# Queries and Fourier inputs in pairs by seven products, values of the latent groups between the first parts of scores, and one modulation tile later

## The chip, the cores and the metric

The kernel runs on one core of one Trainium2 chip, in float32 throughout. The metric is the device time in microseconds of one execution; the time before is the median of three runs.

## The reference

Two models of two layers each run one after the other on 256 tokens of width 1024. The first ("a") has attention, an mLSTM, cross attention and gated FFNs with a short convolution. The change touches almost only the second ("b"), and of it the projections and the attention. In layer 0 of b the latent tokens (256) and the context tokens (256) both go through it, so that its matmuls have 512 columns; in layer 1 only the latent ones ask for queries.

```python
h = modulate(x, lp["g_norm1"], sh1, sc1)
hc = modulate(xc, lp["g_norm1"], modc[..., :d], modc[..., d:2 * d])
proj = h @ lp["w_in"]
projc = hc @ lp["w_in"][:, :n_in_c]
...
c_q, q_g = jnp.split(qc, [MLA_Q_RANK], axis=-1)
q_mla = (rms_norm_2(c_q, lp["g_cq"]) @ lp["w_uq"]).reshape(b, l, MLA_HEADS, MLA_QK)
q_gqa = rms_norm_2(q_g.reshape(b, l, GQA_HEADS, GQA_DIM), lp["g_qn_gqa"])
...
o_mla = blocked_attend(q_mla, jnp.concatenate([k_mla_c, k_mla_l], axis=1),
                       jnp.concatenate([v_mla_c, v_mla_l], axis=1), MLA_QK ** -0.5)
o_gqa = blocked_attend(q_gqa, jnp.concatenate([k_gqa_c, k_gqa_l], axis=1),
                       jnp.concatenate([v_gqa_c, v_gqa_l], axis=1), GQA_DIM ** -0.5)
o_four = fourier_mix(proj[..., FOUR_START:GATE_START])
```

`mod = silu_c @ w_mod + b_mod` gives the shifts, scales and gates of a layer. Its weights are independent of everything in model a.

## The kernel before

The program is one long list of parts, written out by hand; each part names what TensorE, ScalarE, VectorE and GpSimd do in it, and an engine does its pieces in the order of the list. An engine's wait therefore holds up everything behind it on that engine. Results hand over by counters: `tick` raises an engine's counter when an instruction ends, `of` gives the value that a reader waits for.

PSUM has eight banks of 512 float32 columns. Whoever fills a bank again calls `claim(pe, bank)` first, which waits for the labels that the last user left by `lend(bank, ...)`, that is, for its readers.

Weights stream in slabs of up to 32 tiles (128x128) through two slots in turn. SyncE asks for slab g when slab g-2 has been used. `next_tiles` hands the tiles out, and the matmul that ends a slab ticks it.

A linear job (`tensor_linear`, L569) makes 128 output features of 512 columns: eight matmuls, one for each 128 of the 1024 inputs. In the trace each matmul of the program has two records. The first b layer's queries are the jobs 0 to 10 of `q0`: 0 to 2 make the low-rank query (`CQ`), 3 to 6 the grouped queries, of which ScalarE makes the squares (L1561) and VectorE the copy with its gain (`query_reads`, L2343); 7 to 10 are the Fourier inputs, which ScalarE copies half of and VectorE folds (`fold_reads`, L2352 and L2354). The jobs go round the banks 0 to 3. After job 3 the norm of `CQ` (`qnorm0`, L518 to L508) stands on VectorE. Behind `q0` comes `tensor_low` (L2448), which claims banks 0 to 3 in turn.

The merge of this layer, and the FFNs, already multiply a 2x2 block of weights with a 2x2 block of tokens by seven products in place of eight, with sums of weights (GpSimd, L2944; VectorE, L2921 and L2923) and sums of tokens (L2884 and on). A merge unit is one pair of output features (L2799).

The attention of b (`tensor_pairs`, `scalar_pairs`, `vector_pairs`, with the stage names `batt0` and `batt1`) works in units of a pair of heads by 128 queries. Units from `plain` on are the latent ones with rope and go in groups of four score parts (`scores_of_four`, L1356 and L1359), two units u and u+1 at a time. The chain of a unit is: scores on TensorE (banks 2*(u%2) and the next), minima on VectorE, `exps` on ScalarE (L1430), reciprocal and product on VectorE, `turn` on TensorE (L1372, banks 4 and 5), `copy_t` on ScalarE and VectorE (L1448), `values` on TensorE (L1384), and `output` on ScalarE (L1440). The values of a unit go to bank 6 or 7 by the parity of its output number `out`; two units share an output in some families (`out_first`, `out_last`). The first of an output claims the bank, which is lent by the copy of the output two before it. Behind the groups comes a `late` part, the late gate's matmuls (L2784), on TensorE, then the last turns and values.

At the start, `vector_mod_tiles` makes the products for the modulation (L612, two for each tile) between other work of VectorE; each waits for its weights (two transfers of 512 KB) to land in one of three buffers. L1935 (VectorE) and L1947 (TensorE) make the lambda of model a's attention. The tiles 7 and on stand in the jobs of `foxin`, the projection of the first a layer.

## Time and profile before

| | |
|---|---|
| Median of 3 runs | 2502.84 us (2501.11 to 2503.05) |
| The profiled execution | 2505.26 us, span 2503.5 us |
| TensorE busy | 2453.6 us, 98% of the span |
| VectorE, ScalarE, GpSimd busy | 1335.4, 548.7 and 621.4 us |
| Granted TensorE clock, mean | 0.998 |

The span is from the first to the last instruction of the profiled execution; the device time of that execution is 1.8 us longer, and it was 2.4 us slower than the median of the others. TensorE is the engine that the others serve, so a wait on it is time, while waits elsewhere are not.

### The profile page before, as it was taken

To read this page: it belongs to the slowest core of one execution; us is meant where nothing else is said; L and a number is where in the kernel's file an instruction comes from. 1 tells how busy PE (TensorE), PEld (TensorE's weight loads), DVE (VectorE), ACT (ScalarE), POOL (GpSimd) and SP (SyncE) were. 2 spreads that over 40 slices of the span, in tenths; PEclk is the share of its full clock that TensorE was granted. 3 is DMA by queue.
4 is the path that set the end of the run, shared out by engine and by line. 5 is a ranking of instruction groups with operands and counts; after the bars stand their busy time and mean duration, and the time that the engine had idled before them with its cause. 6 is when DMAs were issued, how large, how long until landed. Compare 5 with 4: busy or idle time off the path is not lost.

```text
span 2503.5 us, 37953 instructions
## 1 busy us (share of the span) xinstructions
PE 2453.6 (98%) x14528; PEld 2024.2 (81%) x14528; DVE 1335.4 (53%) x2707; ACT 548.7 (22%) x1199; POOL 621.4 (25%) x536
## 2 busy tenths in 40 slices
PE   9999999999999999999999999999999999999999
PEld 6757889996799999645567767888888875899999
DVE  6676467741325776324836763545542247435775
ACT  2132122111212221214620002222200215212220
POOL 1101135420212544001012221333241010232543
PEclk9999999999999999999999999999999999999999
DMA  8745344433333453120024662121222120243453
GB/s 313 284 186 201 127 162 153 193 131 135 117 135 119 168 193 135 66 87 26 2 84 156 218 260 88 68 101 71 110 93 80 68 95 26 104 166 153 168 193 110
DMA packets 39128, 334.67 MB, mean 134 GB/s; under 512 B 3920, under 2 KB 9168, under 8 KB 21712
## 3 DMA queue, kind: packets, MB, share of 16 engines
q1 hardware_dynamic: 32080, 307.61, 33.0%
q0 software_dynamic: 6912, 25.17, 2.7%
q8 instruction: 95, 1.56, 0.2%
q14 instruction: 41, 0.34, 0.0%
HBM read 331.72 MB, written 1.05 MB: 133 GB/s over the span
## 4 chain that ended last, share of the span: by engine, by line
PE 89%; DVE 5%; DMA 3%; issue 2%; ACT 1%; POOL 1%; SPq 0%; DVEq 0%; POOLq 0%; ACTq 0%
PE PS L767 25%; PE PS L569 15%; PE PS L1016 11%; PE PS L2799 6%; PE PS L1583 4%; PE PS L1743 4%; PE PS L2840 4%; PE PS L1728 3%; PE PS L2318 2%; PE PS L1384 2%; PE PS L1372 1%; DMA arena<-in_mod 1%; PE PS L436 1%; DMA slot<-in_weights 1%; PE PS L748 1%
## 5 line engine op out<-in xcount | busy, mean ns | idle before, releaser
L569 PE MATMUL PS<-XN,slot 128*128 128x256 f32 (+1 forms) x1184 | 296.8, 411 | 0.8 <-DVE XN L508 0.8
L767 PE MATMUL PS<-SQ,slot 128*128 128x128 f32 (+1 forms) x1984 | 294.4, 301 | 1.8 <-DVE slot L859 1.8
L569 PEld LDWEIGHTS PS<-XN,slot 128*128 128x128 f32 x1184 | 224.4, 190 | 69.8 <-issue 42.5
L767 PEld LDWEIGHTS PS<-SQ,slot 128*128 128x128 f32 x1984 | 268.1, 191 | 14.9 <-DVE slot L859 2.0
L1016 PE MATMUL PS<-arena,slot 128*128 128x128 f32 (+1 forms) x1902 | 251.5, 293 | 3.7 <-DVE arena L1094 2.2
L767 PE MATMUL PS<-XN,slot 128*128 128x128 f32 (+1 forms) x1664 | 250.0, 301 | 0.0
L1016 PEld LDWEIGHTS PS<-arena,slot 128*128 128x128 f32 x1902 | 239.1, 192 | 13.5 <-DVE arena L1094 2.8
L767 PEld LDWEIGHTS PS<-XN,slot 128*128 128x128 f32 x1664 | 226.1, 192 | 10.7
L886 DVE SCALAR_TENSOR_TENSOR arena<-PS,small,arena 128x255 f32<-128x255 f32 (+2 forms) x352 | 174.8, 544 | 44.7 <-ACT arena L830 44.1
L830 ACT ACTIVATE arena<-PS,small 128x256 f32<-128x256 f32 (+1 forms) x176 | 105.3, 617 | 399.3 <-DVE PS L919 238.9
L612 DVE CUSTOM_DVE_ANT_0 arena<-arena 128x1024 f32<-128x1024 f32 x80 | 107.3, 1382 | 30.2 <-DMA arena<-in_mod 30.2
L2799 PE MATMUL PS<-arena,slot 128*128 128x256 f32 (+1 forms) x704 | 119.7, 328 | 1.7 <-DVE slot L2923 1.7
L2799 PEld LDWEIGHTS PS<-arena,slot 128*128 128x128 f32 x704 | 107.0, 191 | 11.8 <-DVE slot L2923 2.4
L446 ACT ACTIVATE SQ<-X 128x512 f32<-128x512 f32 (+1 forms) x68 | 36.1, 552 | 364.1 <-DVE X L1058 93.1
L767 PE MATMUL PS<-SQ,probs 128*128 128x128 f32 (+1 forms) x704 | 111.4, 301 | 1.3 <-DVE SQ L871 1.3
L2944 POOL TENSOR_TENSOR slot<-slot 128x512 f32<-128x512 f32 x22 | 30.0, 1364 | 328.9 <-DMA slot<-in_weights 328.9
L612 DVE CUSTOM_DVE_ANT_1 arena<-arena,X 128x1024 f32<-128x1024 f32 x80 | 92.9, 1219 | 33.7 <-DMA arena<-in_mod 33.7
L1743 PE MATMUL PS<-arena,slot 128*128 128x128 f32 (+1 forms) x688 | 110.1, 321 | 0.0
L937 POOL TENSOR_TENSOR slot<-slot 128x512 f32<-128x512 f32 x84 | 108.4, 1291 | 0.0
L1743 PEld LDWEIGHTS PS<-arena,slot 128*128 128x128 f32 x688 | 101.4, 191 | 8.4 <-issue 0.5
L949 POOL TENSOR_TENSOR arena<-arena 128x256 f32 (+3 forms) x88 | 80.6, 916 | 102.6 <-ACT arena L839 102.6
L767 PEld LDWEIGHTS PS<-SQ,probs 128*128 128x128 f32 x704 | 97.7, 191 | 6.0 <-DVE SQ L871 1.5
(302 smaller groups left out, 3828.2 us busy)
## 6 DMA issues: line engine op xcount, KB each, us to landing
slot<-in_weights SPq DMA_DIRECT2D x85, 2048.0 KB, 7.8
slot<-in_weights SPq DMA_DIRECT2D x16, 2816.0 KB, 9.7
slot<-in_weights SPq DMA_DIRECT2D x24, 1536.0 KB, 6.8
arena<-in_mod POOLq DMA_DIRECT2D x48, 512.0 KB, 6.5
arena<-in_mod SPq DMA_DIRECT2D x48, 512.0 KB, 3.3
slot<-in_weights SPq DMA_DIRECT2D x5, 1024.0 KB, 5.5
slot<-in_weights SPq DMA_DIRECT2D x2, 2176.0 KB, 8.4
arena<-in_c SPq DMA_DIRECT2D x2, 1024.0 KB, 12.0
```

The costliest lines, as they stand in the source:

```text
L569: mm = pe.matmul(o, l, r, start=k == 0, stop=k == len(terms) - 1, skip_group_check=True)
L612: return dve.tensor_tensor_reduce(scratch, w, c, 1.0, 0.0, ALU.mult, ALU.add, total)
L767: mm = pe.matmul(PS[:, bank, 0:h], lhs[:, k * P:(k + 1) * P], rhs(k), start=first and k == 0, stop=last and k == 3, skip_group_check=True)
L830: act.activation(hb[:, half, :], src[half], ACT.Identity, bias=conv_col(s, m - 1, half, 3), scale=conv_col(s, m - 1, half, centre))\
L886: op = dve.scalar_tensor_tensor(out=o[:, :, lo:hi], in0=x[:, :, lo + d:hi + d], scalar=conv_col(s, m - 1, half, c), in1=o[:, :, lo:hi], op ...
L937: pool.tensor_tensor(a21, a11, a21, ALU.subtract).then_inc(*w_tick(s, GD, "s3", i, turn))
L949: pool.tensor_tensor(dst, hb[:, 0, :], hb[:, 1, :], ALU.mult).then_inc(*w_tick(s, GD, "h", i, turn))
L1016: mm = pe.matmul(d_psum(p, what, h), lhs[:, k * P:(k + 1) * P], rhs(k), start=k == 0, stop=k == KH - 1, skip_group_check=True)
L1583: mm = pe.matmul(PS[:, bank, 0:cols_n], lhs(k, t), r, start=k == 0, stop=k == k_tiles - 1)
L1743: mm = pe.matmul(PS[:, bank_of(m), part[g]], w[:, a:a + P], rhs(k, part[g]), start=k == 0, stop=k == k_tiles - 1, skip_group_check=True)
L2799: mm = pe.matmul(PS[:, bank, 0:hq], lhs[:, k * P:(k + 1) * P], rhs[:, k, 0:hq], start=first and k == 0, stop=last and k == 3, skip_group_c ...
L2840: mm = pe.matmul(PS[:, BBR + i, 0:nq], slot[:, a:a + P], BR[b][:, k, 0:nq], start=k == 0, stop=k == 3, skip_group_check=True)
```

## The change

There are four edits in one.

1. The modulation tile 7 leaves the start and goes into the `foxin` jobs: `range(0, 7)` there, `range(7, 16)` here.
2. The jobs 5 to 10 of `q0` become three pairs of two output features of 512 columns each, by seven products of four matmuls with 256 columns. GpSimd adds s1 and s3 of each pair's weights in the slab, VectorE s2 and s4; the token sums t1 to t4 are made once by VectorE, ahead of the reads of the first job. Bank 0 or 1 (`ba`) and 2 or 3 (`bd`) hold the products that end in PSUM, 4, 5 and 7 the others. `c12` is made in PSUM, and the reads of the upper job come from bank `ba`, those of the lower one from SBUF. The slab of `q0`'s first jobs is cut short and each pair has a slab of 16 tiles.
3. On TensorE, in both b attentions: the values of u-4 stand between the first score part of u and that of u+1 in each latent group; before, the values of u-2 stood behind the turn of u-1.
4. On ScalarE the output copies follow: those of u-4 and u-3 stand at the end of a group, where those of u-3 and u-2 stood.

```diff
             def scores_of_four(u):
                 for p, rope in enumerate(zip(units[u]["rope"], units[u + 1]["rope"])):
                     for v in (u, u + 1):
+                        if p == 0 and v > u:
+                            values(u - 4)
                         for i in range(2):
                             if p == 0:
                                 claim(pe, 2 * (v % 2) + i)
...
                 turn(u - 2)
-                if u == plain:
-                    values(u - 4)
                 values(u - 3)
                 turn(u - 1)
-                values(u - 2)
-            if plain == n:
-                values(n - 4)
-            else:
+            values(n - 4)
+            if plain < n:
                 late(pe)
...
                 copy_t(u - 1)
-                if u == plain:
-                    output(u - 4)
+                output(u - 4)
                 output(u - 3)
-                output(u - 2)
             copy_t(n - 2)
-            if plain == n:
-                output(n - 4)
+            output(n - 4)
...
-                add(scalar=lambda a: scalar_silu_c(a, 0), vector=lambda d: vector_mod_tiles(d, *range(0, 8)),
+                add(scalar=lambda a: scalar_silu_c(a, 0), vector=lambda d: vector_mod_tiles(d, *range(0, 7)),
...
-                        vector_mod_tiles(dve, *{2: range(8, 16), 6: range(16, 23)}.get(j, ()))
+                        vector_mod_tiles(dve, *{2: range(7, 16), 6: range(16, 23)}.get(j, ()))
...
-                jobs = feature_jobs(xq, lambda k: None, 11, q_reads, segs=qseg)
+                jobs = feature_jobs(xq, lambda k: None, 5, q_reads, segs=qseg)
+                Q_PAIRS = 3
...
+                def tensor_query_pairs(pe, s=s):
...
+                        ba, bd = i % 2, 2 + i % 2
+                        pe.wait_ge(sem, landed)
+                        claim(pe, ba)
+                        product(a11, XQ[:, :, 0, 0:T], ba, last=False).then_inc(*tick(TD, s, "p1", i))
+                        pe.wait_ge(*of(s, "sums", i))
...
+                        claim(pe, 4)
+                        product(s2, TQ[:, 1], 4).then_inc(*tick(TD, s, "p6", i))
+                        claim(pe, 5)
+                        product(s3, TQ[:, 2], 5).then_inc(*tick(TD, s, "p7", i))
+                        claim(pe, bd)
+                        product(s1, TQ[:, 0], bd, last=False).then_inc(*tick(TD, s, "p5", i))
+                        claim(pe, 7)
+                        product(a22, TQ[:, 3], 7).then_inc(*tick(TD, s, "p4", i))
+                        pe.wait_ge(*of(s, "p1_copied", i))
+                        product(a12, XQ[:, :, 1, 0:T], ba, first=False)
+                        pe.wait_ge(*of(s, "c22", i))
+                        product(s4, XQ[:, :, 1, T:2 * T], bd, first=False)\
+                            .then_inc(*tick(TD, "slab", first_slab["pairs0"] + i))
...
+                        lend(ba, (s, "c12", i), *[(s, "read", 5 + 2 * i, r) for r in range(len(upper))])
+                        lend(bd, (s, "c12", i))
...
+                def vector_query_pair(dve, i, s=s):
...
+                    dve.wait_ge(*of(s, "p3", i))
+                    dve.tensor_tensor(PS[:, i % 2, T:2 * T], PS[:, bd, 0:T], Q_U2, ALU.add).then_inc(*tick(VD, s, "c12", i))
+                    for part, made in zip((1, 0), ("c21", "c12")):
+                        dve.wait_ge(*of(s, made, i))
+                        for r, (_, op) in list(enumerate(pair_reads(i)[part]))[1:]:
+                            op(dve).then_inc(*tick(VD, s, "read", 5 + 2 * i + part, r))
```

TensorE at the end of the first jobs of `q0`, before: job 4 (its first row waits for VectorE) and behind it the jobs 5 and 6 in other banks.

```order
L569 MATMUL PS<-XN,slot 128x512 [waits vector_done]
L569 MATMUL PS<-XN,slot 128x512 x7
L569 MATMUL PS<-XN,slot 128x512 [waits scalar_done]
L569 MATMUL PS<-XN,slot 128x512 x7
L569 MATMUL PS<-XN,slot 128x512 [waits vector_done]
L569 MATMUL PS<-XN,slot 128x512 x7
```

The same place after, with lines moved by 6: job 4, then the first products of pair 0 (L2423 is the matmul of `product`).

```order
L575 MATMUL PS<-XN,slot 128x512 [waits vector_done]
L575 MATMUL PS<-XN,slot 128x512 x7
L2423 MATMUL PS<-XN,slot 128x256 [waits vector_done,scalar_done,landed1]
L2423 MATMUL PS<-XN,slot 128x256 x3
L2423 MATMUL PS<-arena,slot 128x256 [waits vector_done]
L2423 MATMUL PS<-arena,slot 128x256 x3
L2423 MATMUL PS<-arena,slot 128x256 [waits vector_done]
L2423 MATMUL PS<-arena,slot 128x256 x3
```

Job 5 waited for ScalarE alone there; the first product of pair 0 waits for VectorE, ScalarE and the landing of its own slab. The last product of pair 2, and the first matmuls of `tensor_low` (now L2581) behind it:

```order
L2423 MATMUL PS<-XN,slot 128x256 [waits vector_done]
L2423 MATMUL PS<-XN,slot 128x256 x3
L2581 MATMUL PS<-arena,slot 128x512 [waits vector_done,scalar_done,landed0]
L2581 MATMUL PS<-arena,slot 128x512
L2581 MATMUL PS<-arena,slot 128x512 [waits vector_done,scalar_done]
```

TensorE in the group of units 16 and 17 of `batt0`, before: the turn of unit 13, the values of unit 12 (L1384 from `probs_t`), then the first score parts of 16 and of 17 (L1356).

```order
L1372 MATMUL PS<-small,probs 128x128 [waits vector_done,scalar_done]
L1372 MATMUL PS<-small,probs 128x128 x3
L1372 MATMUL PS<-small,probs 128x128 [waits vector_done]
L1372 MATMUL PS<-small,probs 128x128 x3
L1384 MATMUL PS<-probs_t,arena 64x128 [waits scalar_done,vector_done]
L1384 MATMUL PS<-probs_t,arena 64x128 x7
L1356 MATMUL PS<-arena 128x256 [waits scalar_done]
L1356 MATMUL PS<-arena 128x256
L1356 MATMUL PS<-arena 128x256 [waits scalar_done]
L1356 MATMUL PS<-arena 128x256
L1359 MATMUL PS<-arena 128x256 x4
```

The same place after (L1380, L1392 and L1364 are the former L1372, L1384 and L1356): the turn, the first part of 16, the values of 12, the first part of 17.

```order
L1380 MATMUL PS<-small,probs 128x128 [waits vector_done,scalar_done]
L1380 MATMUL PS<-small,probs 128x128 x3
L1380 MATMUL PS<-small,probs 128x128 [waits vector_done]
L1380 MATMUL PS<-small,probs 128x128 x3
L1364 MATMUL PS<-arena 128x256 [waits scalar_done]
L1364 MATMUL PS<-arena 128x256
L1392 MATMUL PS<-probs_t,arena 64x128 [waits scalar_done,vector_done]
L1392 MATMUL PS<-probs_t,arena 64x128 x7
L1364 MATMUL PS<-arena 128x256 [waits scalar_done]
L1364 MATMUL PS<-arena 128x256
L1367 MATMUL PS<-arena 128x256 x4
```

The values of unit 12 have gone from in front of the scores of 16 to in front of those of 17. ScalarE in the group of units 14 and 15, before: copy of the turned unit 12, exponentials of 14 and of 15, turned copy of 13, output copy.

```order
L1448 ACTIVATE probs_t<-PS 128x512 [waits tensor_done]
L1430 ACTIVATE probs,pair_sum<-PS,pair_min,query_rstd 128x512 [waits vector_done,tensor_done]
L1430 ACTIVATE probs,pair_sum<-PS,pair_min,query_rstd 128x512
L1430 ACTIVATE probs,pair_sum<-PS,pair_min,query_rstd 128x512 [waits vector_done,tensor_done]
L1430 ACTIVATE probs,pair_sum<-PS,pair_min,query_rstd 128x512
L1448 ACTIVATE rms<-PS 128x512 [waits tensor_done]
L1440 ACTIVATE arena<-PS 128x256 [waits tensor_done]
```

The same place after (L1452, L1434 and L1444 are the former L1448, L1430 and L1440); this output copy is now the one of unit 10, which the values of unit 12 claim their bank from. Before, it was done a group earlier.

```order
L1452 ACTIVATE probs_t<-PS 128x512 [waits tensor_done]
L1434 ACTIVATE probs,pair_sum<-PS,pair_min,query_rstd 128x512 [waits vector_done,tensor_done]
L1434 ACTIVATE probs,pair_sum<-PS,pair_min,query_rstd 128x512
L1434 ACTIVATE probs,pair_sum<-PS,pair_min,query_rstd 128x512 [waits vector_done,tensor_done]
L1434 ACTIVATE probs,pair_sum<-PS,pair_min,query_rstd 128x512
L1452 ACTIVATE rms<-PS 128x512 [waits tensor_done]
L1444 ACTIVATE arena<-PS 128x256 [waits tensor_done]
```

## Rows read from the trace of the kernel before

**Rows 1.** The page: busy time by engine, and the chain that ended last
```profile
PE 2453.6 (98%) x14528; PEld 2024.2 (81%) x14528; DVE 1335.4 (53%) x2707; ACT 548.7 (22%) x1199; POOL 621.4 (25%) x536
...
PE 89%; DVE 5%; DMA 3%; issue 2%; ACT 1%; POOL 1%; SPq 0%; DVEq 0%; POOLq 0%; ACTq 0%
```

**Rows 2.** Timeline of PE, the start (start, length, engine, line, [wait before <-releaser])
```profile
1.46 5.37 PE L2988 MATMUL PS<-rms 128*128 128x512 f32 x6 [1.46 <-DVE rms L3001]
...
68.67 0.35 PE L1947 MATMUL PS<-tiny,small 128*128 128x2 f32 x2 [1.81 <-DVE tiny L1935]
...
158.18 1.13 PE L1344 MATMUL PS<-arena,small 128*128 128x256 f32 x4
```

**Rows 3.** Timeline of DVE (VectorE), the start up to the first attention
```profile
68.36 0.16 DVE L1935 TENSOR_TENSOR tiny<-small 128x2 f32<-128x2 f32 x1
...
153.08 1.23 DVE L612 CUSTOM_DVE_ANT_1 arena<-arena,X 128x1024 f32<-128x1024 f32 x1 [5.98 <-DMA arena<-in_mod]
...
154.24 1.22 DVE L612 CUSTOM_DVE_ANT_1 arena<-arena,X 128x1024 f32<-128x1024 f32 x1
...
159.96 0.29 DVE L1486 CUSTOM_DVE_ANT_0 probs<-PS,small 128x128 f32<-128x128 f32 x1
```

**Rows 4.** Timeline of PE, queries and Fourier inputs, first b layer
```profile
1070.55 48.23 PE L569 MATMUL PS<-XN,slot 128*128 128x512 f32 x112
1118.62 7.03 PE L2448 MATMUL PS<-arena,slot 128*128 128x512 f32 x16
```

**Rows 5.** Timeline of PE, one merge unit and the gate behind it
```profile
1416.91 1.89 PE L2799 MATMUL PS<-XN,slot 128*128 128x256 f32 x8
...
1428.99 7.03 PE L2840 MATMUL PS<-SQ,slot 128*128 128x512 f32 x16
```

**Rows 6.** Timeline of DVE, queries and Fourier inputs
```profile
1071.48 3.35 DVE L521 RECIPROCAL probs_t<-SQ 128x512 f32<-128x512 f32 x1
...
1079.04 1.40 DVE L2343 TENSOR_SCALAR arena<-PS,small 128x512 f32<-128x512 f32 x2
...
1098.70 0.42 DVE L2352 TENSOR_TENSOR arena<-PS,arena 128x256 f32<-128x256 f32 x1 [5.90 <-ACT arena L1561]
```

**Rows 7.** The page: POOL's (GpSimd's) sums, and a weight slab's issue to landing
```profile
L2944 POOL TENSOR_TENSOR slot<-slot 128x512 f32<-128x512 f32 x22 | 30.0, 1364 | 328.9 <-DMA slot<-in_weights 328.9
...
slot<-in_weights SPq DMA_DIRECT2D x5, 1024.0 KB, 5.5
```

**Rows 8.** Timeline of DVE, the first merge unit
```profile
1273.86 0.68 DVE L2921 TENSOR_TENSOR slot<-slot 128x512 f32<-128x512 f32 x1
...
1296.52 0.43 DVE L2915 TENSOR_TENSOR PS<-PS,arena 128x256 f32<-128x256 f32 x1 [3.03 <-PE PS L2799]
```

**Rows 9.** Timeline of PE, groups of four, first b layer's attention
```profile
1211.73 1.13 PE L1356 MATMUL PS<-arena 64*128 64x512 f32 x4 [1.47 <-ACT probs L1430]
...
1227.34 0.70 PE L1356 MATMUL PS<-arena 64*128 64x256 f32 x4 [0.51 <-ACT probs L1430]
...
1242.77 2.34 PE L1356 MATMUL PS<-arena 64*128 64x512 f32 x8
...
1251.41 0.70 PE L1356 MATMUL PS<-arena 64*128 64x256 f32 x4 [0.51 <-ACT probs L1430]
```

**Rows 10.** Timeline of ACT (ScalarE), output copies, first b layer's attention
```profile
1227.57 0.39 ACT L1440 ACTIVATE arena<-PS 128x256 f32<-128x256 f32 x1
...
1244.21 0.66 ACT L1440 ACTIVATE arena<-PS 128x256 f32<-128x256 f32 x2
```

**Rows 11.** Timeline of PE, groups of four, second b layer's attention
```profile
2103.86 1.13 PE L1356 MATMUL PS<-arena 64*128 64x512 f32 x4 [0.80 <-ACT probs L1430]
...
2132.13 1.09 PE L1384 MATMUL PS<-probs_t,arena 128*64 128x128 f32 x16
2133.15 3.72 PE L2784 MATMUL PS<-XN,slot 128*128 128x256 f32 x16
```

**Rows 12.** Timeline of ACT, the output copy before the late gate's end
```profile
2134.58 0.39 ACT L1440 ACTIVATE arena<-PS 128x256 f32<-128x256 f32 x1
```

109 lines of the change are left out of this document (104 added, 5 removed).

## Prediction

> **What bounds the kernel now.** I read the page first. TensorE is busy for 98% of the span and carries 89% of the chain that ended last [rows 1]: time is saved only by taking matmuls away from TensorE or by shortening one of its few waits, and every new wait on it is paid in full, unless it eats one that stood behind it. Then I read TensorE's timeline at the four places that the change touches, then VectorE's and ScalarE's rows at the same places, because each wait there ends with a semaphore of one of those two, and last the order of instructions, to see behind what the released instruction now stands.
>
> **Part A, the moved modulation tile.** At 68.67 TensorE waited 1.81 us for the small product at L1935 on VectorE [rows 2], which started at 68.36, directly behind the last modulation tile [rows 3]. A tile is two instructions of the kind at 153.08 and 154.24, which start 1.16 apart, so 2.3 us [rows 3]. With tile 7 gone from there the product comes 2.3 us sooner and the wait of 1.81 goes whole: at most -1.8. But VectorE is then one tile behind until it catches up. Up to the first attention it does not: the tiles are bound by their landings, and the last group (tiles 30 to 32) starts when it has waited 5.98 us for a landing, at 153.08, and ends as the first minimum of the attention starts, at 159.96 [rows 3]. The scores that this minimum reads ended at about 159.3 (158.18 + 1.13) [rows 2]. Now the group is four tiles if the landings don't come sooner: the minimum would be at about 162.2, +2.3; if they come sooner (their buffers and the queue follow TensorE's slabs, which are 1.8 earlier), it is at about 158.3 and all is kept. Both ends: -1.8 and +0.3 (a part of the lag is absorbed, as attention's first exponentials hold two units of scores in reserve). I take **-1.0**, past the middle towards the gain, since nothing shows the landings to be late by themselves.
>
> **Part B, three pairs by seven products.** Before, seven jobs took 48.07 us, from 1070.55 to 1118.62 [rows 4], 6.87 each, so the six that are replaced took 41.2. A pair does 7 products x 4 matmuls with 256 columns each, exactly what a merge unit does between its start at 1416.91 and its next other work at 1428.99 [rows 5]: 12.08 us, three times 36.24. Gain of matmul time: **-4.96**.
>
> What is given back at the seams. *Entry:* the first product of pair 0 claims bank 0, which job 4, the matmuls just before it, filled. Bank 0 is free when VectorE has read it, and that read (the second of the two at 1079.04, ending 1080.44) stands behind the norm of the queries: the reciprocal of 3.35 us from 1071.48 and what follows it [rows 6]. Job 4's matmuls end 6.87 after 1070.55, at 1077.42. So TensorE stands 3.0 us and some semaphore time: **+3.1**. Before, job 5 went to another bank and nobody noticed. *Exit:* the low-rank stage at L2448 started without a wait [rows 4], because the last job was in bank 2; its first matmul wants bank 0, which pair 2 (banks 0 and 2) lends when its last sum c12 is made in PSUM (0.43, as at 1296.52 [rows 8]) and when VectorE, behind the two folds of the lower job, has done the two of the upper (folds of 0.42, as at 1098.70, starting 0.35 apart [rows 6]): 0.2 to notice + 4 x 0.35 + 0.42 = **+2.05**. *Inside the pairs* nothing waits: GpSimd's two sums are 1.36 us each [rows 7] and VectorE's two 0.69 each [rows 8], under 5 us in all against 12.08 of matmuls, and the slab of 16 tiles (1024 KB, 5.5 us to landing [rows 7]) is asked for when the slab two before is done, 12 us or more ahead. If that cover were gone, a pair would pay up to the 5.5. For pair 0 the two sums stand behind the same reads, and are ready at 1080.44 + 1.4 = 1081.9, while the first product runs until 1080.5 + 1.7 = 1082.2: just hidden, by 0.3. The four token sums (four of the 128x1024 kind, 1.2 us each by the tile rows [rows 3]) go to VectorE between 1055 and 1061, where it had nothing to do before the first query read. Part B: -4.96 + 3.1 + 2.05 = **+0.2**. So what seven products save is paid at the two seams.
>
> **Part C, values of the latent groups, first attention.** The values of unit u-4 now stand between the first part of the scores of u and that of u+1. The second part waits for the exponentials of u-1, since they free its banks: 1.47 at 1211.73 and 0.51 at 1227.34 and 1251.41 [rows 9]. In the first group of four this fills a wait: values of 1.02 in place of standing, but ScalarE then becomes the next bound, so I take **-0.65** of the 1.47 (0 and -1.0 as ends). In the later groups the same work only changes its side of the wait, so nothing is gained. And the output copies on ScalarE have moved too: the copy of unit u-4 now stands behind both exponentials and the turned copy of its group. Three of the moved values (units 12, 16, 18) are the first of their output bank and claim it: they wait for the copy of units 10, 14 and 16. In the program the claim asks for a later ScalarE count than the second part of the scores does. Where was that copy in time? In the trace of before the copy that stands in the same place, behind exponentials and turned copy, ended at 1227.57 + 0.39 = 1227.96; at the second place there are two in one row at 1244.21, of which the first, the one that is waited for, ends after the same 0.39, at 1244.60 [rows 10]. Then the values need 1.02 (from 2132.13 to 2133.15 [rows 11]), with 0.07 of semaphore, and the scores behind them start at 1229.06, against 1227.34; at the second place at 1245.7, against 1243.95, where the second half of the row at 1242.77 began (2.34 long, 0.12 of it wait) [rows 9]; the third, at 1251.41, repeats the first. **+1.7 three times, +5.2.** The price is that of a matmul group behind a claim on the engine's one queue: the scores, the ropes and both turns of the group are queued behind it, and ScalarE's next exponentials wait for them, so nothing gives it back. Part C: **+4.6** (ends -0.65 and +5.2).
>
> The Trainium skill ("Perfetto Trace Analysis", the section on a TensorE instruction's phases) says that TensorE's queue can pull weight loads ahead of matmuls in flight and reorders nothing else; by it the scores can't pass the values that wait. If they could, the term of 5.2 would be nothing and the sum 1.2. The trace agrees as far as it can: the matmul row at 1211.73 stands 1.47 with all that is behind it.
>
> **Part D, the second attention.** The first group gains out of the wait of 0.80 at 2103.86 [rows 11]: -0.55, and two small waits of 0.12 are filled, or not: I give +0.24 for them on account of the output copies. Its values of unit 12 stood in front of the late gate's matmuls at 2133.15 [rows 11] and now stand behind a claim that is released by the copy at 2134.58 + 0.39 = 2134.97 [rows 12]: + 1.02 + 0.07 = 2136.07 against 2133.15, **+2.9**. The late gate follows it and waits too. Part D: **+2.6** (ends -0.35 and +2.9).
>
> **The sum.** -1.0 + 0.2 + 4.6 + 2.6 = +6.4. It is made in the profiled execution, 2505.26 us, which is 2.4 above the median of the runs (2502.84); put on the median it gives **2509.2** (0.26% slower). Its own range is 2506.5 to 2511.5: A between -1.8 and +0.3, C and D together within 1.5. I call 0.2% (5.0 us) what a measurement of this kernel can tell.
>
> **The rivals.** *No late outputs:* if the copies don't hold the values up (ScalarE reaches them sooner, because its exponentials start sooner once the first part of the scores is no longer behind values), C and D are -0.65 and -0.35: -1.0 + 0.2 - 1.0 = -1.8, 2501.0. For it: the first part of the scores does start 1.02 sooner. Against: the exponentials of u-1, which are what ends last, hang on the group before and not on it. *Half of it:* the copies cost in the first attention alone or with half the price: -1.8 + 2.9 to -1.8 + 5.2, 2504 to 2506.5. *Hand-over free, faster:* a single mechanism, banks given back before they are asked for, at the seams of the pairs as well as for the outputs: -1.0 - 4.96 - 1.0 = -7.0, 2495.9. It decides from the point at which VectorE's read of job 4 ends before 1077.4; it ended at 1080.44, and for that the norm of the queries would have to be out of its way. *The clock falls:* the granted clock is 0.998 over the run, and no row shows what happens behind a new stand of 3 us in a full stretch. The start shows the lower level (1.2 GHz): six matmuls with 512 columns took 5.37 [rows 2], where 48.23 / 112 = 0.43 each [rows 4] makes 2.6, so 2.8 us for a drop; at both seams +5.6, 2514.8. The stands of 1.81 [rows 2] and 1.47 [rows 9] left the mean at 0.998. The Trainium skill ("TensorE: Matmul & The Clock Gate", "A second HAM failure mode: psum-queue depth-cycling") says that many small pauses between groups which go round the PSUM banks can drop the clock too. That would be the whole of attention, and no row of this trace shows it: the matmuls behind the waits of [rows 9] are no longer than those at 1242.77, which follow none.
>
> **How the numbers follow.** Main case .55, no late outputs .14, half of it .14, hand-over free .05, clock falls .07, other .05. The predicted time is the main case's. The range reaches down to the no-late-outputs case (2501.0) and up to 2513, short of the clock's 2514.8, and leaves out the hand-over and the clock cases and half of the rest, .15. Slower by over 0.2% (above 2507.8): .50 of the main case, the clock, .01 of the rest, .58. Faster: .06. Within 0.2%: .36.
>
> **What would show it.** A: no wait at L1947's row, and VectorE's first minimum against the end of the first scores. B: a wait of about 3.1 before the first of L2423, released by VectorE's query read; 36.3 from there to the last; a wait of about 2.0 before L2581. No wait inside: if one is seen, on GpSimd's sums or a slab, that step is wrong. C: three waits before L1392, ended by ScalarE's L1444, with the scores' wait behind it gone. D: one of about 2 us before the late gate. Were the values' waits under 0.5 each, C and D would be wrong; were there no wait at the pairs' entry, B would be.

## The result, and the profile after

The changed kernel takes 2525.8 us in the median of six executions (2515.75 to 2527.73), the kernel before 2502.7 in the same rounds (2501.11 to 2507.78): a ratio of 1.0082, interval 1.0068 to 1.0097. The forecast was 2509.2 with a range up to 2513. The direction was right; the size was 23 us where 6.4 were forecast. The profiled execution took 2525.13 us, with a span of 2523.3 against 2503.5, and a mean granted clock of 0.995 against 0.998: 19.8 us to account for.

First the waits of TensorE in the changed kernel, grouped by the waiting line and what released it (us in total, times, the longest):

```profile
PE PS L1392 <- ACT arena L1444: 8.1, 4, 2.8
PE PS L1350 <- DVE pair_min L1487: 7.6, 1, 7.6
...
PE PS L2932 <- ACT probs L2993: 3.9, 1, 3.9
...
PE PS L2423 <- DVE arena L2344: 3.0, 1, 3.0
...
PE PS L1364 <- ACT probs L1434: 2.9, 9, 0.9
...
PE PS L2581 <- DVE arena L2355: 2.0, 1, 2.0
```

Each row adds up one kind of wait. The first, the fourth and the last are the waits that the prediction put there: the values (L1392) for an output copy, the first product of pair 0 (L2423), the low-rank stage (L2581). The second and the third, 7.6 us before a unit's scores in the very first attention and 3.9 in the merge, are in no term of it.

The start, on TensorE. It answers to [rows 2]:

```profile
66.71 0.28 PE L1948 MATMUL PS<-tiny,small 128*128 128x2 f32 x2
...
158.93 1.13 PE L1350 MATMUL PS<-arena,small 128*128 128x256 f32 x4
167.63 0.80 PE L1350 MATMUL PS<-arena 64*128 64x128 f32 x4 [7.57 <-DVE pair_min L1487]
...
170.66 2.07 PE L1350 MATMUL PS<-arena,small 128*128 128x256 f32 x4
```

and on VectorE, answering to [rows 3]:

```profile
149.33 1.23 DVE L618 CUSTOM_DVE_ANT_1 arena<-arena,X 128x1024 f32<-128x1024 f32 x1 [4.16 <-DMA arena<-in_mod]
...
163.99 1.23 DVE L618 CUSTOM_DVE_ANT_1 arena<-arena,X 128x1024 f32<-128x1024 f32 x1 [5.41 <-DMA arena<-in_mod]
...
166.29 0.29 DVE L1487 CUSTOM_DVE_ANT_0 probs<-PS,small 128x128 f32<-128x128 f32 x1
```

The lambda matmul is 1.96 us sooner and waits no more. But VectorE makes four tiles (28 to 31) from 149.33 and then stands 5.41 us for the landing of the last one, tile 32, at 163.99. A tile's weights come in one transfer of 512 KB (the trace has one issue for each tile, and both products read it), not in two. When it was asked for is in GpSimd's timeline, and when the next weight slab was in that of SyncE's queue:

```profile
154.29 0.53 POOL L643 DMA_DIRECT2D arena<-in_mod  x1 [1.77 <-DVE modulation L618]
```

```profile
153.49 0.33 SPq L3155 DMA_DIRECT2D slot<-in_weights  x1
```

Tile 32 was asked for 0.8 us behind the slab and took 9.7 us to land. The first minimum starts at 166.29, where [rows 3] have 159.96, and the third unit's scores wait 7.57 for it. Behind that wait, four matmul records with 256 columns take 2.07 us where the same row before the wait takes 1.13: the granted clock has fallen. From 167.63 to the start of the first row of eight records of L1350 it is 10.03 us, where the kernel before takes 6.82 for the same matmuls (162.00 to 168.82), so 3.2 us come on top of the wait.

The pairs and the low-rank stage behind them, answering to [rows 4]:

```profile
1085.18 2.99 PE L2423 MATMUL PS<-XN,slot 128*128 128x256 f32 x8 [3.01 <-DVE arena L2344]
...
1125.41 7.10 PE L2581 MATMUL PS<-arena,slot 128*128 128x512 f32 x16 [2.05 <-DVE arena L2355]
```

The first row is p1 of pair 0: 2.99 us for the eight records that take 1.89 in [rows 5]. The attentions, answering to [rows 9] and [rows 11]:

```profile
1234.27 1.09 PE L1392 MATMUL PS<-probs_t,arena 128*64 128x128 f32 x16 [1.90 <-ACT arena L1444]
...
1252.60 1.08 PE L1392 MATMUL PS<-probs_t,arena 128*64 128x256 f32 x8 [1.47 <-ACT arena L1444]
...
1261.72 1.09 PE L1392 MATMUL PS<-probs_t,arena 128*64 128x128 f32 x16 [1.90 <-ACT arena L1444]
...
2149.71 1.09 PE L1392 MATMUL PS<-probs_t,arena 128*64 128x128 f32 x16 [2.83 <-ACT arena L1444]
2150.73 5.41 PE L2917 MATMUL PS<-XN,slot 128*128 128x256 f32 x16
```

Four values stand for a copy, and the late gate's first sixteen records take 5.41 us where [rows 11] have 3.72. In the merge, TensorE and, below, VectorE:

```profile
1471.06 3.16 PE L2932 MATMUL PS<-XN,slot 128*128 128x256 f32 x8 [3.94 <-ACT probs L2993]
```

```profile
1467.62 2.31 DVE L618 CUSTOM_DVE_ANT_0 arena<-arena 128x1024 f32<-128x1024 f32 x1 [3.90 <-DMA arena<-in_mod]
...
1469.86 0.42 DVE L3048 TENSOR_TENSOR PS<-PS,arena 128x256 f32<-128x256 f32 x1
```

The sum c12 (L3048), and ScalarE's read behind it, stand behind a tile of the second layer's modulation that waits for its landing. And the clock, in windows of 5 us (the last three numbers are granted clock, DMA share and GB/s):

```profile
165.00:170.00 5.00, 2.37 (x10) 1.95 (x12) 4.15 (x23) 2.48 (x11) 0.00 (x0) 0.50 0.06 24
...
1085.00:1090.00 5.00, 4.82 (x15) 3.95 (x16) 1.32 (x3) 0.39 (x1) 2.49 (x2) 0.66 0.26 108
1090.00:1095.00 5.00, 5.00 (x25) 4.41 (x24) 1.27 (x3) 0.00 (x0) 0.00 (x0) 1.00 0.00 0
...
1470.00:1475.00 5.00, 3.94 (x11) 3.21 (x12) 4.54 (x8) 0.98 (x2) 0.00 (x0) 0.67 0.49 147
...
2150.00:2155.00 5.00, 5.00 (x28) 4.04 (x25) 0.01 (x1) 0.00 (x0) 0.00 (x0) 0.66 0.02 5
```

A window at 0.66 has granted 5 x (1 - 0.66) = 1.7 us less than full speed: that is the price of one fall to 1.2 GHz where TensorE has matmuls throughout. Summed over all windows the changed kernel was granted 11.9 us less (5.1 at 164 to 175, 1.7 each at 335, 1085, 1470 and 2150) and the kernel before 5.1 (1.7 at 190, 3.4 at 325 to 335), without the windows at the very end. Not all of that is time: the fall of 5.1 began at 164.4, and what lay in the wait, up to 167.63, cost nothing more.

The 19.8 us by stretch, each from the start of the same matmul in both traces:

| up to | before | after | later by | added in the stretch |
|---|---|---|---|---|
| lambda matmul | 68.67 | 66.71 | -1.96 | -2.0 |
| third unit's scores | 162.00 | 167.63 | +5.63 | +7.6 |
| query norm's matmuls | 1067.98 | 1072.57 | +4.59 | -1.0 |
| low-rank stage | 1118.62 | 1125.41 | +6.79 | +2.2 |
| late gate, first b layer | 1258.50 | 1269.82 | +11.32 | +4.5 |
| groups of four, second b layer | 2101.93 | 2116.79 | +14.86 | +3.5 |
| late gate, second b layer | 2133.15 | 2150.73 | +17.58 | +2.7 |
| end of the span | 2503.5 | 2523.3 | +19.8 | +2.2 |

Five rows answer to terms of the forecast: C (+4.6 forecast, +4.5 measured), D (+2.6, +2.7), B (+0.2, +2.2, of which 1.7 is the clock), and the first two rows together A (-1.0, +5.6). The -1.0 of the third row hides the 3.2 us of slow matmuls behind the late start: the kernel before had its own fall at 190, which the changed one had not, and lost 1.4 us more at 328. The last row is the clock behind the late gate, 1.7 of 2.2 (5.41 against 3.72). The 3.5 of the stretch that holds the merge had no term.

### The profile page after: what moved, and what is told of

Same layout as the page of the kernel before. It is cut to its first block, busy times and chain, and to the rows that moved or that the text cites. A ratio compares the mean times of both kernels' runs of the same rounds, so it can differ in the third digit from the quotient of the medians.

```text
span 2523.3 us, 38148 instructions
## 1 busy us (share of the span) xinstructions
PE 2454.5 (97%) x14600; PEld 2041.1 (81%) x14600; DVE 1348.9 (53%) x2732; ACT 549.4 (22%) x1202; POOL 626.3 (25%) x542
## 4 chain that ended last, share of the span: by engine, by line
PE 85%; DVE 6%; DMA 4%; issue 2%; ACT 1%; POOL 1%; SPq 0%; DVEq 0%; POOLq 0%; ACTq 0%
PE PS L773 25%; PE PS L1022 11%; PE PS L575 10%; PE PS L2932 6%; PE PS L1584 4%; PE PS L1744 4%; PE PS L2973 4%; DMA arena<-in_mod 3%; PE PS L1729 3%; PE PS L2319 2%; PE PS L1392 2%; PE PS L2423 2%; DVE arena L618 1%; PE PS L442 1%; PE PS L1380 1%
## 5 line engine op out<-in xcount | busy, mean ns | idle before, releaser
L575 PE MATMUL PS<-XN,slot 128*128 128x256 f32 (+1 forms) x1088 | 255.6, 395 | 0.8 <-DVE XN L514 0.8
L575 PEld LDWEIGHTS PS<-XN,slot 128*128 128x128 f32 x1088 | 206.1, 190 | 46.9 <-issue 19.6
L773 PEld LDWEIGHTS PS<-XN,slot 128*128 128x128 f32 x1664 | 226.1, 192 | 10.7
L2932 PEld LDWEIGHTS PS<-arena,slot 128*128 128x128 f32 x704 | 107.6, 192 | 12.7 <-DVE slot L3056 3.1
```

Of the source, the lines that this page charges most:

```text
L575: mm = pe.matmul(o, l, r, start=k == 0, stop=k == len(terms) - 1, skip_group_check=True)
L773: mm = pe.matmul(PS[:, bank, 0:h], lhs[:, k * P:(k + 1) * P], rhs(k), start=first and k == 0, stop=last and k == 3, skip_group_check=True)
L2932: mm = pe.matmul(PS[:, bank, 0:hq], lhs[:, k * P:(k + 1) * P], rhs[:, k, 0:hq], start=first and k == 0, stop=last and k == 3, skip_group_c ...
```

## The experiments

All times are medians, beside the kernel before in the same rounds, and the ratio has its 95% interval. Of the kernel before the medians were 2505.05 in the first four experiments' rounds, 2504.65 in the next four, 2506.05 in the next four and 2504.14 in the last three.

**The tile alone.** The kernel before, with

```diff
-vector_mod_tiles(d, *range(0, 8))
+vector_mod_tiles(d, *range(0, 7))
...
-{2: range(8, 16), 6: range(16, 23)}
+{2: range(7, 16), 6: range(16, 23)}
```

> The kernel before with the modulation tile moved and nothing else. Theory one (the last tile, 32, stands alone with one of three buffers, lands behind a weight slab and holds VectorE's first minimum): the wait of 1.8 us at the lambda product is gone, TensorE waits about 7.6 us before the third unit's scores and runs below full clock behind it; in all +5 to +7 us against before. Rival (the wait in the changed kernel came from a chance in how transfers met and not from the tile): -1.8 us, first minimum within 0.5 us of the end of the first scores.

2508.77, ratio 1.0006 (0.999 to 1.0021). The profiled execution has a wait of 10.50 us before the third unit's scores and was at 2514. But the twelve times fall in two heaps: five between 2501.5 and 2502.9, seven between 2507.5 and 2516.6. So the late start comes with the tile alone, and by the times not in every execution. By this run alone the tile could not be told from chance: the interval holds 1, and the kernel before has a tail up to 2516 too.

**The pairs alone.** The kernel before with the new slabs, jobs and pairs; no tile, values or copies moved.

> The kernel before with the three pairs alone; tile, values and outputs as before. Theory one: matmuls 4.96 shorter, 3.0 of wait at the entry, 2.05 at the exit, and about 1.8 more because the granted clock falls behind the entry's wait: +1.5 to +2.5 against before. Rival one (the clock's fall was not of this wait): +0.2. Rival two (the pairs shift the slabs and by that the modulation's landings in the merge): a wait of over 3 us in the merge, +5 or more.

2510.15, ratio 1.0014 (1.0 to 1.0028): +5.1. Waits of 3.00 at the entry and 2.04 at the exit, and the clock loses 1.7 behind each. From the query norm to the low-rank stage it is 52.84 us against 50.64, +2.2. The merge has a wait of 3.32 and a fall of 1.7, as the second rival said.

**Values and output copies alone.** The kernel before with those two moves.

> The kernel before with the values and the output copies moved in both attentions; tile and jobs as before. Theory one: three waits of 1.5 to 1.9 us in the first attention and one of 2.8 in the second for an output copy, +4.5 and +2.7, and about 1.7 for the clock behind the wait of 2.8: +7 to +9 against before. Rival (the waits come from the time at which attention starts in the changed kernel): under +3.

2517.78, ratio 1.005 (1.003 to 1.007), +12.7 from six executions. The four waits are as in the changed kernel (1.91, 1.48, 1.90, 2.83), the first groups to the late gate take 53.84 us where the kernel before takes 49.37, and one fall of the clock follows the last. That explains 9 of the 12.7, which is above what was expected. The profiled execution, the second slowest of the six, also had a late start of 6.2 us, with the tile at its old place; how many of the others had one is not shown. The rival, that the four waits come from the time at which attention starts, falls.

**The entry's wait alone.** The kernel before, and only

```diff
+                jobs[5]["needs"] = {(0, 0): [(s, "read", 4, 1)]}
```

> The kernel before, in which job 5 of the queries also waits for VectorE's read of job 4, as the first product of pair 0 does; nothing else. It measures the entry's wait by itself. Theory one: 3.0 us of wait, and the matmuls behind it run at the lower clock until they have lost 1.7 to 1.9 us: +4.8 against before. Rival (a wait of 3 us does not change the clock): +3.1, the matmuls of job 5 as long as all others.

2510.37, ratio 1.0018 (1.0007 to 1.0028), +5.3. Nothing is computed differently. The profiled execution has the wait of 3 us and a fall of the clock behind it, 4.8 us together:

```profile
1078.56 43.13 PE L569 MATMUL PS<-XN,slot 128*128 128x512 f32 x96 [3.01 <-DVE arena L2343]
```

```profile
1075.00:1080.00 5.00, 1.99 (x5) 0.71 (x4) 3.40 (x5) 0.60 (x1) 0.00 (x0) 0.91 0.00 0
1080.00:1085.00 5.00, 5.00 (x10) 2.06 (x9) 0.00 (x0) 0.00 (x0) 0.00 (x0) 0.75 0.00 0
1085.00:1090.00 5.00, 5.00 (x13) 2.28 (x12) 0.75 (x1) 0.60 (x1) 0.00 (x0) 1.00 0.00 0
```

0.91 and 0.75 make 0.45 + 1.25 = 1.7 us, with 10 records of 512 columns in the window at 0.75 and 13 in the next. 96 records at 0.43 would be 41.3 and are 43.1. So the fall needs nothing of the pairs. The median agrees, but can't decide alone: its interval, +1.8 to +7.0, holds the rival's +3.1 too. And the fall isn't certain: the same wait stands in the changed kernel, e2, e5 and e9, and in e9 no fall follows it.

**The output copy sooner.** The changed kernel with

```diff
                 copy_t(u - 2)
+                output(u - 4)
                 exps(u)
                 exps(u + 1)
                 copy_t(u - 1)
-                output(u - 4)
                 output(u - 3)
```

> The changed kernel with one line moved: ScalarE copies the output of u-4 ahead of the exponentials of its group and not behind them. The values stay between the score parts. Theory one (the late copies make the four waits for the output bank, and the clock's fall in the second attention hangs on the last of them): the waits of 1.9, 1.5, 1.9 and 2.8 us are gone, the first attention is 5.3 us shorter than in the changed kernel and the second 2.8, and the lower clock behind the late gate's start goes, 1.7: -9 to -11 against the changed kernel's 2525.8, so about 2516. Rival (the values in front of the second score part cost by their place): under -3.

2513.75, ratio 1.0024 (1.0008 to 1.004): 12 below the changed kernel's median. All four waits are gone from the profile; the second attention:

```profile
2131.34 1.09 PE L1392 MATMUL PS<-probs_t,arena 128*64 128x128 f32 x16
2132.36 3.72 PE L2917 MATMUL PS<-XN,slot 128*128 128x256 f32 x16
```

No wait before the values of unit 12, and the late gate is back at the 3.72 of [rows 11]. So the whole loss of C and D, 7.2 us and 1.7 of clock, was in the place of one copy of 0.39 us. The pairs' seams still stand there (3.01 and 2.05). That the median fell 3 us further is not shown to be the copy's doing: the times lie in two heaps, four up to 2507.3 and eight from 2512.6 on, and the profiled execution, of the lower one, had no late start.

**The pairs on other banks.** The pairs alone, so that job 4 and pair 0, and pair 2 and the low-rank stage, meet in different banks; VectorE makes the first weight sums ahead of the query norm. The main lines of the edit:

```diff
-                        ba, bd = i % 2, 2 + i % 2
+                        ba, bd = 1 - i % 2, 2 + i % 2
...
+            if l == 0:
+                add(vector=lambda d: vector_pair_sums(d, 0))
             add_norm_aside(f"qnorm{l}", [dict(
...
+            LOW = (0, 3, 1, 2)
...
-                    claim(pe, m)
+                    claim(pe, LOW[m])
```

> The pairs alone, on other banks: pair 0 and 2 in banks 1 and 2, pair 1 in 0 and 3; the sums of pair 0's weights stand ahead of the query norm on VectorE; the low-rank stage fills banks 0, 3, 1, 2 in that order. Theory one: no wait at the entry, under 0.5 at the exit, no fall of the clock at either: 3.0 + 1.7 + 3.4 = about 8 us less than the pairs alone (2510.2), so 2502 and 3 us below the kernel before of the same rounds. Rival (something else in the pairs costs, the merge's landings by the shifted slabs): 2505 or more, with the wait of over 3 in the merge still there.

2502.51, ratio 0.9988 (0.9972 to 1.0004): 7.6 below the pairs alone, and 2.1 below the kernel before, which is within the noise. TensorE, over the whole stretch:

```profile
1067.18 7.03 PE L575 MATMUL PS<-XN,slot 128*128 128x512 f32 x16
1074.04 1.89 PE L2428 MATMUL PS<-XN,slot 128*128 128x256 f32 x8
...
1106.85 3.62 PE L2428 MATMUL PS<-XN,slot 128*128 128x256 f32 x16
1110.30 7.03 PE L2589 MATMUL PS<-arena,slot 128*128 128x512 f32 x16
```

From 1074.04 to 1110.30 it is 36.26 us, the 36.24 of the sum; in this stretch the matmuls' gain of 4.96 is now kept whole. The wait in the merge is still there, 3.79, with 3.4 us of lower clock: the rival was right in that part. It is enough to explain why the median gained 2 and not 5, but no run took it away alone.

**The lambda product first.** The kernel before, in which VectorE's `products` stand ahead of the eight tiles, and the rest of `vector_start` where it stood.

> The kernel before, in which VectorE makes the lambda product ahead of all eight modulation tiles; no tile moves. It has what the moved tile was to gain without the tile. Theory one (the tile's place decides): wait at the lambda matmul gone, -1.8 to -2.3, and no more late starts of the first attention than in the kernel before: -2 in the median. Rival (TensorE starting 2 us sooner is by itself what makes the first minimum late, since the landings don't come sooner): 0 to +4, with a wait in front of the third unit's scores as in the tile alone.

2503.71, ratio 0.9989 (0.9973 to 1.0006), 0.9 below. The wait before the lambda matmul is gone, and in the profiled execution no late start followed; the median's gain is half of what was expected and not clear of noise.

**All repairs.** The lambda product first, tile 7 at its old place, the pairs on the other banks, the values between the scores with the early copy.

> All repairs together: lambda product first and tile 7 at its old place, the pairs on the other banks, the values between the score parts with the early output copy. Theory one: -2 + -4.5 + -1 = 7 to 8 us below the kernel before of the same rounds, 2497 to 2498. Rival (chance in the landings swamps it): within 2 us of the kernel before.

2498.85, ratio 0.9972 (0.9957 to 0.9987): 5.8 below the kernel before, 27 below the changed kernel. The gain is 0.28%, the interval lies wholly below 1, and 7 to 8 us had been expected.

**The tile back.** The changed kernel with `range(0, 8)` and `range(8, 16)` again.

> The changed kernel with tile 7 back at its old place. Theory one (the moved tile makes the late first minimum of the first attention frequent: 6 of 12 executions of the tile alone are about 10 us above the others): the executions of this kernel lie mostly 8 to 10 us below the changed kernel's 2525.8, median 2516 to 2520. Rival (the late start is chance, as frequent with the tile at its old place): median within 3 us of 2525.

2518.53, ratio 1.005 (1.003 to 1.0071), some 7 below the changed kernel, within what was expected, though from seven executions and other rounds. (The expectation counts six late executions of the tile alone; there are seven.) Its profiled execution has a late start too, of 2.87 us: with the tile at its old place the late start is rarer, not gone.

**The kernel before once more.**

> The kernel before, unchanged, profiled once more. It shows how far its waits and the places of lower clock differ from one execution to the next. Theory one: the waits on other engines are the same to 0.1 us, those behind landings differ by 1 to 3 us, and each fall of the clock costs 1.7 us or a multiple of it. Rival (the profile of before is typical in each wait): no difference over 0.3 us anywhere.

2504.98, ratio 1.0003 (0.9992 to 1.0014). This execution lost nothing to the clock. The same matmuls after the same wait, first in the kernel before as profiled, then in this run:

```profile
328.14 10.29 PE L748 MATMUL PS<-XN,slot 128*128 128x128 f32 x64 [2.79 <-DVE XN L508]
```

```profile
325.51 8.53 PE L748 MATMUL PS<-XN,slot 128*128 128x128 f32 x64 [2.67 <-DVE XN L508]
```

A wait of 2.7 us is followed by a lower clock in one execution and not in the next. The matmuls took 1.8 us longer, though the clock was granted 3.4 less: 0.7 of the fall lay in the wait, and the first sixteen of the 64 records are up to 0.21 apart at full clock too, as far as at the lower one. And the start of this run, on VectorE:

```profile
149.85 1.22 DVE L612 CUSTOM_DVE_ANT_1 arena<-arena,X 128x1024 f32<-128x1024 f32 x1 [4.14 <-DMA arena<-in_mod]
...
159.02 0.28 DVE L1486 CUSTOM_DVE_ANT_0 probs<-PS,small 128x128 f32<-128x128 f32 x1
```

Here four tiles (29 to 32) are made without a pause from 149.85, none waits for a further landing, and the first minimum started a microsecond sooner than in [rows 3].

**The slabs alone.** The kernel before, with the last two slabs of the query stage cut into four of 16 tiles.

> The kernel before with the last two slabs of the query stage cut in four of 16 tiles, as the pairs need them; no pairs. In all five profiles with pairs the merge holds a wait of 2.7 to 3.9 us for the late c12 sum, in the five without it no wait there is over 1.7. Theory one (the two more slabs shift the later transfers): a wait of over 2.5 us in the merge, and +2 to +4 against before. Rival (it comes from the pairs' own instructions, or is chance): merge waits under 1.7, no difference to before.

2504.63, ratio 1.0 (0.9983 to 1.0016). The longest of the merge's waits for c12 is 1.41, and the median is the kernel before's. The slabs by themselves don't make the merge's longer wait; the theory falls. The profiled execution had a late start of 5.88 us, with the tile at its old place.

**Values early, alone.** The kernel before with the values moved and the early copy.

> The kernel before with the values between the score parts, and ScalarE's output copy of u-4 ahead of the exponentials. Theory one: no wait for an output bank; of the waits of 1.47 and 0.80 for the exponentials in the first groups 1.0 and 0.6 are filled, the two of 0.51 go: -1.5 to -2 us against the kernel before. Rival (the copy ahead of the exponentials delays them by its 0.4 in each group): 0 to +2.

2505.21, ratio 0.9995 (0.9985 to 1.0005). No wait for a bank, and 48.90 us in place of 49.37 over the first attention's groups, 31.05 in place of 31.22 over the second's: 0.6 us gained in the trace, a third of what was expected, and nothing that the median can tell. With the first waits filled, small ones of 0.2 and one of 0.89 stay, each ended by the exponentials.

**Two tiles.** The kernel before with `range(0, 6)` and `range(6, 16)`.

> The kernel before with two modulation tiles (6 and 7) moved behind the lambda product, twice the suspected lag. Theory one (each tile of lag makes it likelier that the last tile lands after one more weight slab, and then the first attention starts 8 to 10 us late): nearly all executions late, median +8 or more against before of the same rounds. Rival (the late start is chance, whatever the lag): a share of late executions as in the kernel before, median within 2 us.

2513.04, ratio 1.0029 (1.0015 to 1.0043), +8.9. Only one execution of each kernel is profiled, so for the others a late start is judged by the time. All nine times lie at 2507.6 or above; of the 26 of the kernel before in these rounds five do. VectorE, then TensorE:

```profile
163.72 1.22 DVE L612 CUSTOM_DVE_ANT_1 arena<-arena,X 128x1024 f32<-128x1024 f32 x1 [6.21 <-DMA arena<-in_mod]
164.87 1.22 DVE L612 CUSTOM_DVE_ANT_1 arena<-arena,X 128x1024 f32<-128x1024 f32 x1
166.02 0.28 DVE L1486 CUSTOM_DVE_ANT_0 probs<-PS,small 128x128 f32<-128x128 f32 x1
```

```profile
167.36 0.80 PE L1344 MATMUL PS<-arena 64*128 64x128 f32 x4 [8.09 <-DVE pair_min L1486]
```

It is the changed kernel's start again, and by the times now in every execution. The last tiles and the slab are asked for in the same order as there:

```profile
150.93 0.53 POOL L637 DMA_DIRECT2D arena<-in_mod  x1 [5.38 <-DVE modulation L612]
153.22 0.53 POOL L637 DMA_DIRECT2D arena<-in_mod  x1 [1.76 <-DVE modulation L612]
```

```profile
152.72 0.33 SPq L3022 DMA_DIRECT2D slot<-in_weights  x1
```

Tile 31 was asked for at 150.93, 1.8 us ahead of the slab, and had landed 3.8 us later. Tile 32 was asked for at 153.22, half a microsecond behind the slab, and landed 10.5 us later.

This reading can be made in every profile, since each has the same slab at this point. The last tile's request against the slab's, how long the transfer took, and what followed:

| profile | asked for | landed after | VectorE stood | first minimum | third unit's scores waited |
|---|---|---|---|---|---|
| e10, tile in place | 2.1 us ahead of the slab | 3.4 | - | 159.02 | - |
| e15, tile moved | 0.5 ahead | 3.5 | - | 159.44 | - |
| e9, in place | 0.4 ahead | 6.1 | 1.86 | 163.57 | 2.87 |
| e11, in place | 0.1 ahead | 8.9 | 4.64 | 168.23 | 5.88 |
| e13, two moved | 0.5 behind | 10.5 | 6.21 | 166.02 | 8.09 |
| e3, in place | 0.8 behind | 8.3 | 4.03 | 168.29 | 6.20 |
| changed kernel, moved | 0.8 behind | 9.7 | 5.41 | 166.29 | 7.57 |
| e1, moved (its tile 31) | 0.5 behind | 10.6 | 6.38 | 168.79 | 10.50 |

The nine other profiles asked for tile 32 between 1.2 and 8.3 us ahead of that slab (e5, with the tile moved, 1.4), and in none did VectorE stand for it. A load that was asked for behind the slab, or as good as with it (e11), landed 0.2 to 0.7 us behind the slab. So the late start hangs on which of two transfers is asked for first. A moved tile puts one tile more of VectorE's work, 2.3 us, ahead of the last request; it shifts the odds and does not decide alone: e5 and e15 have it and are in time, e3, e9 and e11 haven't and are late.

**One tile sooner.** The kernel before with `range(0, 9)` and `range(9, 16)`.

> The kernel before with tile 8 made ahead of the lambda product too: the opposite move. Theory one: the lambda matmul waits some 5 to 7 us longer, for tile 8 and its landing, and the late starts become rare; the lambda wait costs +5 to +9. Rival (the same chance of a late start): the same cost, and a tail of executions 8 to 10 us above it.

2508.47, ratio 1.0017 (1.0007 to 1.0028). The lambda matmul waits 4.4, 2.6 more than the 1.8 of [rows 2], and a fall of the clock of 1.7 follows: +4.3, less than the +5 to +9 expected. Eleven of the twelve times lie between 2505.2 and 2510.0, one at 2514. The tail is nearly gone.

**All repairs but the tile.**

> All repairs but one: the pairs on the other banks and the early output copies, with the start of the changed kernel, the moved tile. Compared with the version that makes the lambda product first (2498.85, -0.28%). Theory one (the lag decides): late starts in about half of the executions, median 2501 to 2508. Rival (the moved tile is harmless): median 2497 to 2500, no more outliers.

2507.42, ratio 1.0002 (0.9987 to 1.0017), against 2498.85 with the lambda product first: +8.6. Four times lie at 2502.4 or below, eight at 2506 or above; of the twelve with the product first, one lies above 2502. The two kernels differ in how the lambda wait goes away, by the moved tile or by the product's place, and the moved tile is much the dearer way. The heaps speak for the late start as the reason; the profiled execution, of the lower heap, had none and can't show it.

## Why the prediction was wrong

**Part A failed, and it is the largest miss.** The step was "Now the group is four tiles if the landings don't come sooner: the minimum would be at about 162.2", with the ends -1.8 and +0.3. It counted one tile more in the last group, 2.3 us of VectorE, and did not ask whether that tile would be in the group. There are three buffers, and tile 32 is asked for when tile 29 has been used. In [rows 3] it was asked for at 147.40, long before the next slab, and had landed when VectorE came to it. In the changed kernel it was asked for at 154.29, behind the slab of 153.49, and VectorE stood for it until 163.99. So the price is not one tile but one landing: the first minimum came 6.3 us later, at 166.29, the third unit's scores 5.6 later, and 3.2 us of slow matmuls followed. A was forecast at -1.0 and measured +5.6 up to those scores. Two tiles of lag make it in every execution, by the times (e13), one tile in seven or eight of twelve (e1, e5, e15), none now and then (e3, e9 and e11 as profiled), and one tile less hardly ever (e14). What the bounds lacked was the shape of the price, a jump and not a slope. "Nothing shows the landings to be late by themselves" was wrong on its face: the 5.98 us of [rows 3] is VectorE waiting for one, asked for 1.0 us behind the slab before.

**Part B: mechanism and sizes right, one term missing.** 36.24 for the matmuls (36.26 in e6), 3.1 at the entry (3.01), 2.05 at the exit (2.05), nothing inside the pairs. That the exit fits to the hundredth is luck: its terms add up to 2.02, and the 0.2 among them is in no row. What the sum lacked is the lower clock behind the waits, 1.7 us in the changed kernel and 3.4 in e2. This was the rival "the clock falls", at a chance of .07 and with 2.8 us for a drop, worked out from the start; it is 1.7, and behind the entry's wait it came in four of five profiles.

**Part C and D: right.** +4.5 and +2.7 against +4.6 and +2.6, by waits of 1.90, 1.47, 1.90 and 2.83 for the output copies; e5 takes them away by the copy's place alone. The gain of the move itself, put at 0.65 and 0.35, measured 0.5 and 0.2 with the copy out of the way (e12). Missing is again the clock behind the last wait, 1.7.

**The merge was not looked at**, since no edit touches it. The stretch that holds it added 3.5 us: its longest wait is 3.94 where the kernel before has 1.39, and a fall of 1.7 follows. There the c12 sum stands on VectorE behind a tile that waits for its landing. VectorE's own wait is nearly the same in both, 3.90 and 3.71 us (the second at 1452.89); what differs is how long TensorE has to stand for it. In the seven profiles of kernels with pairs TensorE's longest such wait was 3.9, 3.3, 2.9, 3.8, 2.7, 3.2 and 2.0; in the ten without, 1.4 to 2.1. So it goes with the pairs, though not cleanly. It isn't the slabs alone (e11), and it isn't the entry's wait (e4, 1.6). Which part of the pairs does it stays open: shown is the difference, not its way.

**The rivals and the sum.** "Hand-over free" is what e5 and e6 built on purpose, and it gives the -5 of the matmuls in their stretch, though not in the median. The step that failed in the other parts is that each new wait was priced at its length. The trace of before had in [rows 2] to [rows 12] no matmul behind a wait of 3 us, and that the stands of 1.81 and 1.47 "left the mean at 0.998" was taken as a sign against a fall; the 0.002 that was missing from 1 was 5 us in two places, and a query of the clock by windows would have shown the fall behind the 2.79 at 328.14.

The Trainium skill ("TensorE: Matmul & The Clock Gate", "HAM oscillation — how this bites in real kernels") says that long enough idle gaps between matmuls bring the clock down, and that the loss comes on top of the wait. The order of events agrees: e4 has the wait of 3.0, then the fall, then 1.7 us of loss. As to what is long enough the page asks for a longer gap than several that sufficed here (2.0 us in e2 and e9, 2.7 in many), so that by it most of the waits behind which it fell would have had no clock term; the measurement decides.

The median of the changed kernel is near the sum of its parts: 3.7 for the tile, 5.1 for the pairs and 12.7 for values and copies make 21.5, against 23.1. The fit is better than its terms: the tile's interval includes no effect at all, and the 12.7 has 3.7 in it that no wait of the values explains.

## What to carry to other kernels

Price a new wait of TensorE of about 3 us at its length and 1.7 us more, a shorter one at its length and a chance of that, and look at the granted clock in windows before saying what existing waits cost. When a piece of work is moved behind others that are bound by landings, count in landings and not in its own length: ask when the last item is asked for, and ahead of or behind which transfer. When matmuls move past others, check for each that claims a bank where on the other engine the copy stands that gives the bank back; here one copy of 0.39 us, behind two units' exponentials, cost 9 us and, ahead of them, nothing.

## What the runs showed of the hardware

**The size of a fall.** In all 17 profiles every fall of the granted clock, the last microseconds of the span left out, takes 1.7 us of clock or a multiple of it (3.4, 5.1, 6.8). It costs that much time where TensorE has matmuls throughout: 0.45 + 1.25 in e4, 5.41 against 3.72 for the late gate's first sixteen records. It costs less where part of it lies in the wait (164.4 to 167.63 in the changed kernel) or where the matmuls were held up anyway: at L748 3.4 us of it cost 1.8 (10.29 against 8.53), and 1.7 us of it, in the changed kernel, 0.4 (8.89).

**How often it falls.** Counted over the 17 profiles, the first and last 10 us of each left out, a fall began during a wait of TensorE or within 2.2 us behind it in 3 of 188 waits of 1 to 1.5 us, 5 of 19 of 1.5 to 2, 6 of 12 of 2 to 2.6, 12 of 17 of 2.6 to 2.8, 10 of 13 of 2.8 to 3.5, and in all 8 longer ones. The same wait can do either: behind the 3.0 us of the pairs' entry it fell in the changed kernel, e2, e4 and e5, not in e9; behind the 1.9, 1.5 and 1.9 of the first attention in e9, not in the changed kernel nor in e3.

**A small load behind a large one.** A load of 512 KB that was asked for 0.5 to 2.1 us ahead of a slab of 2 MB took 3.3 to 3.8 us (e4, e5, e7, e8, e10, e15, and tile 31 of e13); asked for 0.5 to 0.8 us behind it, 8.3 to 10.6 us (e1, e3, e13 and the changed kernel), and it landed 0.2 to 0.7 us behind the slab. In between, 0.1 and 0.4 us ahead, it took 8.9 (e11) and 6.1 (e9).

The kernel before has therefore a spread of its own, from 2499.7 to 2516.1 us over its executions in these rounds. Falls of the clock are one part of it that its two profiles show (5.1 us in one, none in the other). Late starts are likely another: its profiles have none, but those of e3, e9 and e11, with the same start, have.
